# Loading an expert's first weight matrix with one transfer of two blocks instead of two transfers of one

## What is computed

```python
s = sigmoid(u @ w_router)                       # 512 tokens, 64 experts, 8 picked per token
w = 2.5 * s[picked] / sum(s[picked])
for e in range(64):
    t = tokens that picked e                    # 64 on average
    gate, up = split(u[t] @ w_exp_up[e])        # w_exp_up[e]: 1024 x 512
    acc[t] += w[t, e] * ((silu(gate) * up) @ w_exp_down[e])   # w_exp_down[e]: 256 x 1024
out = x + acc + shared_expert(u)
```

## Time and profile before

| | |
|---|---|
| median of 3 runs | 1250.26 us (1250.15 to 1260.4) |
| profiled execution, own time | 1251.38 us |
| its span | 1249.2 us |
| PE busy | 1146.9 us (92%) |
| DVE busy | 902.0 us (72%) |
| ACT busy | 725.6 us (58%) |
| POOL busy | 262.5 us (21%) |
| DMA | 285.58 MB, mean 229 GB/s |

### The profile page before, as it was taken

The page is one execution under the profiler, slowest core; times in us unless marked ns, Lnnn a source line. Parts: engine busy times, 40 slices in busy tenths (PEclk is TensorE's granted clock), DMA queues, the critical chain, the costliest instruction groups (busy, mean ns, idle before and its releaser), DMA issues.

```text
span 1249.2 us, 16254 instructions
## 1 busy us (share of the span) xinstructions
PE 1146.9 (92%) x5693; PEld 863.5 (69%) x5693; DVE 902.0 (72%) x1133; ACT 725.6 (58%) x926; POOL 262.5 (21%) x145
## 2 busy tenths in 40 slices
PE   4999998999999899798999999999999999999993
PEld 3699987766777788675676666666666666666662
DVE  4576378544433585576899889888888898989881
ACT  7543333334333322412788787878787788888771
POOL 1000000000000000001233344443334444434331
PEclk9999999999999999898999999999999999999997
DMA  6323231221111423524899999999999999999982
GB/s 222 120 59 94 84 97 64 70 65 52 49 60 41 164 68 117 204 118 161 312 358 358 356 368 369 369 365 368 366 364 371 363 369 375 379 366 367 367 293 32
DMA packets 74494, 285.58 MB, mean 229 GB/s; under 512 B 10868, under 2 KB 33416, under 8 KB 49620
## 3 DMA queue, kind: packets, MB, share of 16 engines
q1 hardware_dynamic: 59716, 251.16, 53.8%
q0 software_dynamic: 14736, 33.87, 11.3%
HBM read 272.39 MB, written 29.38 MB: 242 GB/s over the span
## 4 chain that ended last, share of the span: by engine, by line
PE 45%; DMA 32%; DVE 11%; ACT 7%; issue 4%; SPq 0%; POOL 0%; DVEq 0%; ACTq 0%; POOLq 0%
PE bank L1428 35%; DMA arena<-in_w_exp_up_dram 27%; DVE split L1331 5%; ACT split L538 4%; DMA out_dram<-arena 3%; PE bank L1596 2%; PE bank L1623 2%; PE bank L1507 1%; ACT arena L538 1%; PE bank L1741 1%; DMA arena<-u_rows,arena 1%; PE bank L1608 1%; DVE gatheredT L1338 1%; DVE arena L1161 1%; DMA arena<-in_x_dram 1%
## 5 line engine op out<-in xcount | busy, mean ns | idle before, releaser
L1331 DVE TENSOR_TENSOR split<-arena,split 128x2048 fp32r<-128x2048 f32 x192 | 437.7, 2287 | 60.0 <-ACT split L538 59.2
L1428 PE MATMUL bank<-split,gatheredT 128*96 128x512 f32 x1536 | 374.0, 399 | 26.5 <-DVE gatheredT L1338 25.9
L538 ACT ACTIVATE split<-arena 128x2048 fp32r<-128x2048 f32 x192 | 367.3, 1919 | 48.0 <-DMA arena<-in_w_exp_up_dram 48.0
L1428 PEld LDWEIGHTS bank<-split,gatheredT 128*96 128x96 f32 x1536 | 244.7, 163 | 137.3 <-issue 32.1
L500 POOL DMA_INDIRECT arena<-u_rows,arena x64 | 134.9, 2107 | 603.5 <-DVE arena L1325 572.0
L508 POOL DMA_INDIRECT out_dram<-arena x64 | 121.6, 1899 | 367.9 <-ACT arena L538 286.6
L1428 PE MATMUL bank<-split,hidT 128*96 128x512 f32 x768 | 191.9, 398 | 1.5 <-ACT arena L538 1.5
L1428 PEld LDWEIGHTS bank<-split,hidT 128*96 128x96 f32 x768 | 119.0, 162 | 47.0 <-issue 1.6
L1428 PE MATMUL bank<-hT_high,front_split 128*128 128x512 f32 x448 | 146.4, 408 | 0.8 <-DVE hT_low L870 0.8
L538 ACT ACTIVATE arena<-bank 96x512 f32<-96x512 f32 (+4 forms) x217 | 107.8, 533 | 64.5 <-PE bank L1428 29.2
L1428 PEld LDWEIGHTS bank<-hT_high,front_split 128*128 128x128 f32 x448 | 83.2, 193 | 28.7 <-issue 11.5
(11 more groups left out here) (245 smaller groups left out, 1245.3 us busy)
## 6 DMA issues: line engine op xcount, KB each, us to landing
arena<-in_w_exp_up_dram SPq DMA_DIRECT2D x128, 1024.0 KB, 14.3
arena<-in_w_exp_down_dram SPq DMA_DIRECT2D x64, 1024.0 KB, 14.3
arena<-in_w_in_dram SPq DMA_DIRECT2D x14, 1024.0 KB, 5.4
arena<-in_w_in_dram SPq DMA_DIRECT2D x10, 768.0 KB, 4.5
arena<-in_w_branches_dram SPq DMA_DIRECT2D x4, 1024.0 KB, 5.0
arena<-in_w_out_dram SPq DMA_DIRECT2D x4, 1024.0 KB, 5.1
arena<-in_x_dram SPq DMA_DIRECT2D x4, 512.0 KB, 4.9
arena<-in_w_mem_kv_dram SPq DMA_DIRECT2D x2, 1024.0 KB, 5.1
```

The source lines that it names most:

```text
L538: return nc.scalar.activation(o, i, ACT.Copy, **kw)
L1331: v.tensor_tensor(both[:, 1], raw[q % RAW], both[:, 0].bitcast(F32), ALU.subtract).then_inc(low_done, 1)
L1428: ins = mm(bank, left[a], right[b], start=first and q == 0, stop=last and q == 2)
```

## The change

The two blocks of the first product are loaded by one transfer. Their source becomes 16384 contiguous bytes per partition, and the destination is one view over two ring buffers that lie side by side (`raw_up`). For this the order of the six buffers is changed, so that blocks 0 and 1 of either expert are neighbours and the down blocks take places 4 and 5. The transfer waits until both buffers are free, that is, until the second block of the expert two before has been converted, and signals the first block's semaphore alone; ACT waits on it for both blocks. The conversion, products, gathers and scatters are not touched. At the start the pair of the second expert waits for the shared expert's second weight block (S0 + 2).

```diff
-        raw = [at(ring_at + 2048 * n, 4, 512) for n in (2, 3, 4, 5, 0, 1)]
+        raw = [at(ring_at + 2048 * n, 4, 512) for n in (2, 3, 4, 0, 1, 5)]
+        raw_up = [view(arena[:, o:o + 4096], 4096) for o in (ring_at + 4096, ring_at)]
...
-            up_src = io["w_exp_up"][0].rearrange("e (p j k) n -> p e j (k n)", p=P, j=2)
+            up_src = io["w_exp_up"][0].rearrange("e (p k) n -> p e (k n)", p=P)
...
             def load_expert(e, n, u0):
 
-                for j in range(BLOCKS):
-                    load_expert_block(e, n, j, u0)
-
-            def load_expert_block(e, n, j, u0):
-                s = (BLOCKS * n + j) % RAW
-                if not isinstance(u0, int) or u0 + j >= RAW:
-                    sp.wait_ge(low_done, u0 + (j - RAW + 1))
-                elif s < 4:
+                load_up(e, n, u0)
+                load_down(e, n, u0)
+
+            def load_up(e, n, u0):
+                s = BLOCKS * n % RAW
+                if not isinstance(u0, int) or u0 >= RAW:
+                    sp.wait_ge(low_done, u0 + (2 - RAW))
+                elif s == 0:
                     sp.wait_ge(x1_done, 2 * NT)
                 else:
-                    sp.wait_ge(front_low, S0 + s - 3)
-                if j < 2:
-                    sp.dma_start(raw[s].rearrange("p k n -> p (k n)"), up_src[:, e, j, :]).then_inc(raw_in[s], 16)
+                    sp.wait_ge(front_low, S0 + 2)
+                sp.dma_start(raw_up[n % 2], up_src[:, e, :]).then_inc(raw_in[s], 16)
+
+            def load_down(e, n, u0):
+                s = (BLOCKS * n + 2) % RAW
+                if not isinstance(u0, int) or u0 >= RAW:
+                    sp.wait_ge(low_done, u0 + (3 - RAW))
                 else:
-                    sp.dma_start(raw[s].rearrange("p k n -> p (k n)"), dn_src[:, e, :]).then_inc(raw_in[s], 16)
+                    sp.wait_ge(x1_done, 2 * NT)
+                sp.dma_start(raw[s].rearrange("p k n -> p (k n)"), dn_src[:, e, :]).then_inc(raw_in[s], 16)
 
             load_expert(0, 0, 0)
             load_expert(1, 1, 3)
-            load_expert_block(2, 2, 0, 6)
-            load_expert_block(2, 2, 1, 6)
+            load_up(2, 2, 6)
...
-            load_expert_block(2, 2, 2, 6)
+            load_down(2, 2, 6)
             load_expert(3, 3, 9)
...
-                act.wait_ge(raw_in[q % RAW], round0 * 16 + 16 * (q // RAW + 1))
+                act.wait_ge(raw_in[q % RAW - (q % BLOCKS == 1)], round0 * 16 + 16 * (q // RAW + 1))
                 copy(split[q % SPLIT][:, 0], raw[q % RAW]).then_inc(high_done, 1)
```

## The result

The changed kernel takes 1291.3 us (median of 4 runs, 1287.95 to 1298.86) against 1250.24 before: a ratio of 1.0335, 95% interval 1.0305 to 1.0364. It is slower by 41 us, where 28 were forecast. The profiled execution is the slowest of the four, 1298.86 us with a span of 1296.6; on another chip the same kernel ran at 1287.3 us, 1.0314 (1.0286 to 1.0342).

A forecast was written before the change was run, and what follows sets the result against it. The full weights' stream bounds the kernel, with the serial scatters nearly as long. Sharing 3.84 + 0.83, scaled for resting engines, gives a 10.5 us period: +0.50 x 57 = +28, other terms 0, about 1280 us; range 1245 to 1326.

The forecast's parts named there:

- Three loops: Expert loop, 9.97 us per period: DMA share 1.02, PE 9.5 us plus short hand-overs, serial scatters 9.86 us.
- slack for the scatter: Expert loop: the scatters' serial loop of 9.86 us has 0.11 us to spare against the 9.97 us period.
- its loop as the new bound: After the change the serial scatters set the period: 10.5 us, +0.50 over 9.97.
- engines that rest part of each period: DMA engines' work needs 9.97 us of a longer period, so they rest and sharing is scaled by the busy part.
- The signs to look for: 16 KB packets, scatters landing at 9.8 us or more, mostly waiting for landings, DMA share near 0.95, period near 10.5, PE near 90%.
- Part 3: Weights' packets: one of 16 KB takes 0.61 us; merging saves 4 to 10 us if the stream alone sets the pace.
- Part 4: Scatter's turns on the DMA engines: waiting behind 16 KB instead of 8 KB packets adds 0.83 us per scatter.
- The even count of the earlier trace: With both queues active, 76 weights' packets and 65 of the scatter's queue went through, so engines take turns by packet.
- sharing: Part of each scatter's landing due to sharing engines with the weights: 3.84 us beyond the 5.26 us without them.
- part 1: Up weights' load: one issue fewer gains nothing, the first block's issue 4.2 us later costs 0 while the queue is full.
- Part 2: ACT's first copy waits for all 2 MB: +3 us once if the stream is the bound, 0 if the scatters are.
- the stream would run dry: Rival: the pair is issued too late and the weights' stream stops each time; 1280 us too, chance 0.06.

The follow-up runs named there:

- e4: Changed kernel, but odd experts' results go to a second HBM buffer, so a scatter waits for the one two experts before: 1253.7 us, ratio 1.0022.
- e1: Changed kernel's 2 MB transfer, late issue and single landing, but the two buffers are not neighbours, so pieces are 8 KB: 1281.9 us, ratio 1.0270.
- e3: Changed kernel, but two 1 MB transfers with 8 KB pieces, issued once both buffers are free, each block converted on its own landing: median 1268.6 us, ratio 1.0068.
- e5: e3 plus one wait: the first block is converted only when the second has landed too; 1274.3 us, ratio 1.0198.
- e9: Changed kernel with each low part on DVE cut into four instructions of a quarter length: 1277.2 us, ratio 1.0198.
- e11: e1 (2 MB transfer, 8 KB pieces) with each low part on DVE cut into four instructions: 1267.3 us, ratio 1.0135.
- e8: Changed kernel with each low part on DVE cut into two instructions of half length: 1282.0 us, ratio 1.0234.
- e6: Kernel before, but each 1 MB transfer moves two 4 KB pieces per partition instead of one of 8 KB: 1252.1 us, ratio 1.0013.
- e7: Kernel before, but each 1 MB block of the first product comes by two 0.5 MB transfers with 4 KB pieces: 1254.1 us, ratio 1.0042.
- e10: Kernel before with each low part on DVE cut into four instructions: 1251.0 us, ratio 0.9998.

## Why the prediction was right, and where it was not

**The place was right.** Three loops close together, hardly any slack for the scatter, its loop as the new bound, engines that rest part of each period: the chain shows it, and e4 shows it by relaxing that one wait. (The slack is 0.07 us rather than 0.11: from a landing to the next start it is 639.52 - 629.89 - 8.83 = 0.80 us, not 0.76.) The signs to look for came out as said: 52 of 64 scatters waited for a landing, PE at 91%, a period of 10.78 (10.55 in the second chip's profile) where I had 10.5, DMA share 0.94 to 0.99 where I had about 0.95. The landing did not quite reach my 9.8: 9.7, and 9.5 in the second profile. The median hides part of it: the 47 landings among these periods that the next scatter waited for averaged 9.97.

**Part 3, the packets, was right.** From 530 to 538 us the queue moved 3.40 MB in 320 packets, 33 of them tiny, at a share of 100.8%:

```profile
q1 hardware_dynamic: 320, 3.40, 100.8%
```

The 287 others are 128 of 16 KB and 159 of 8 KB by their bytes; 129.0 us of engine time less 159 x 0.314 leaves 0.62 us for one of 16 KB, as extrapolated (0.61). Its saving came to nothing visible.

**Part 4 was mis-sized in what it was for.** I put all 0.83 us per scatter on the pieces. Between the changed kernel and e1 they cost 5 to 9 us, 0.1 to 0.16 us per period, and the rest of a landing after the issue grew by 0.06 to 0.18 us. The even count of the earlier trace rows is true, but that each turn passes on its whole length does not follow: 4 KB pieces took 0.26 us off that rest, half of what the turns would give. And the 3.84 us that I called sharing were not all that: the landing of 5.26 us at 1227.48 has an issue of 1.42 us, the loop's mean is 1.92, so 0.5 us of the difference was POOL waiting for DVE, a wait that my sum did not have and that grew by 0.39 us with the change.

```profile
1227.48 1.42 POOL L508 DMA_INDIRECT out_dram<-arena  x1 [7.04 <-ACT arena L538]
```

**Parts 1 and 2, costed at 0, are where the larger part came from.** By the ratios: late issue alone 0.7% (8 us, loosely fixed), joint landing 1.3% (16 us), one transfer instead of two 0.7% (9 us), pieces 0.45 to 0.65% (5 to 8 us). That these add up to the 39 to 41 proves nothing, since each is the step from one run to the next on one path from before to changed. In another order the shares may differ: the joint landing without the late issue, for one, was not run, and by the medians the first two are 18 and 6. My check of part 1 asked only whether the stream would run dry, and was right in that: e3's share is 1.02, e4's too. What it left out is that the computation's place in time against the stream matters to a loop with so little slack. Part 2 said "0 if the scatters are the bound"; the profile of e5 has 0.29 us more per period than that of e3 in that very case, of which only 0.08 is a longer issue. So the total of 28 us came out near 41 because one term was too large and others missing, not because the sum was right.

**The gathers** I had left out. They share POOL, its queue and its issue with the scatters; when scatters run late, the gather behind them lands late too, and PE waits (53.4 us in 28 waits, and 43.7 in 33 in the second profile; 21.3 in 18 waits in e3, 29.4 in 22 in e5, 42.5 in 37 in e1).

**Open:** by what path the late issue, the joint landing and the single transfer cost what they do. Longer issues are part of it, as e9 and e11 show (10 to 15 us), but the rest of the landing's growth has not been tied to one cause. A rival that no run sets apart is the way over PE: late gathers, waits, then TensorE at its lower clock, results late for their scatter. It has at least the 4 to 10 us of scatters that waited for a result. That DMA rests in e5 (share 0.99) may be effect as well as cause.

## What to carry to other kernels

Before merging transfers, look for a serial loop that shares their engines and compare its length with the period: here 9.90 against 9.97 us, so that little was needed for it to become the bound, 57 times over. Merging saves a fixed part per packet that a full queue hardly shows (420 GB/s with 1 MB transfers before, 425 after), and gives up an early issue, an early landing and an even rhythm. If an indirect DMA from POOL is in such a loop, look at what DVE runs when it is issued. A second destination, so that a scatter waits for the one two before, took away 38 of the 41 us here, but e4 leaves out adding the two together, which has a cost that was not measured.

## What the hardware showed that I had not expected

- POOL's issue of an indirect DMA, 1.3 to 1.4 us, is held up by a running DVE instruction with two SBUF inputs until that instruction ends: up to 3.5 us in all.
- Loads to 64 partitions each, with 16 KB pieces, run at far less than one load to 128: 232 GB/s in the loop against 341 in the changed kernel, ratio 1.29 for the kernel.
- After a wait of 5.4 us for a gather (712.1 to 717.5), TensorE's clock was granted at its lower level (1.2 GHz) for part of the next 8 us, and twelve matmuls took 4.97 us instead of 2.79; columns as in the earlier trace rows, the clock before the last two:

```profile
716.00:724.00 8.00, 6.48 (x23) 4.74 (x23) 3.22 (x3) 2.67 (x3) 0.79 (x1) 0.57 0.85 298
724.00:732.00 8.00, 8.00 (x43) 5.79 (x42) 5.09 (x5) 6.83 (x9) 4.39 (x2) 1.00 0.84 287
```

So idle time on PE cost more than itself. Between 640 and 1225 us of the changed profile the lower level was granted eight times, 44 us in all, and each time it began during a wait of PE for a gather (1.7 to 7.1 us long) or right behind one. That makes the granted 0.97 of the windows after, where before it was 1.00 throughout. In other profiles it was 38 us (second chip), 27 (e5), 21 (e1 and e8), 17 (e9), 7 (e3), 3 (e4 and e11) and 0 (before, e6, e7, e10).
